# Gate sums of a product-key layer formed in PSUM: two products of 128 columns in place of one of 256, and one copy in place of copy and add

## The reference

```python
s = jnp.einsum('thpd,hpnd->thpn', q, sub_keys)            # 8 heads, 2 x 128 sub-keys
vals, idx = lax.top_k(s, K)                               # K = 16
cand = vals[:, :, 0, :, None] + vals[:, :, 1, None, :]
top_s, top_pos = lax.top_k(cand.reshape(T, PEER_HEADS, K * K), K)
experts = (i1 * PEER_NKEYS + i2).reshape(T, PEER_HEADS * K)
gates = jax.nn.softmax(top_s, axis=-1).reshape(T, PEER_HEADS * K)
a = jax.nn.gelu(jnp.einsum('td,ted->te', xb, u_tab[eb]), approximate=False)
y = jnp.einsum('te,ted->td', gb * a, v_tab[eb])
```

## Time and profile before

| | |
|---|---|
| median of 3 runs | 3389.28 us |
| the profiled execution | 3415.09 us, its span 3413.2 us |
| PE busy | 3196.7 us, 94% of the span |
| DVE busy | 2390.1 us, 70% |
| ACT busy | 1105.3 us, 32% |
| POOL busy | 997.1 us, 29% |
| sweep 1's products | 774.5 to 2276 us |
| groups of gates | 796.7 to 2039 us |

### The profile page before, as it was taken

One profiled execution on the slowest core, in us unless ns is written; L12 is line 12 of the kernel. 1 busy time (PEld: TensorE's weight loads), 2 busy tenths in 40 slices (PEclk: granted clock), 3 DMA queues, 4 the chain that ended last, 5 costly groups with the idle time before them and its releaser, 6 DMA issues. The chain is left out here.

```text
span 3413.2 us, 44800 instructions
## 1 busy us (share of the span) xinstructions
PE 3196.7 (94%) x14706; PEld 2637.1 (77%) x14706; DVE 2390.1 (70%) x4021; ACT 1105.3 (32%) x1301; POOL 997.1 (29%) x727
## 2 busy tenths in 40 slices
PE   4993999998999999999999999997998998999996
PEld 3872677887888888888888888876887886788885
DVE  5345343458878878788787873425887888888887
ACT  3123145113333333333333331122333334333333
POOL 0000010002323223232232320024554557755651
PEclk9995579999999999999999999998999999999998
DMA  6500022222333333333343333237999998999995
GB/s 243 190 30 32 1 81 99 74 80 87 146 140 129 116 134 146 140 132 117 129 152 140 139 118 133 100 142 262 352 349 352 352 360 323 372 364 355 348 362 192
DMA packets 251409, 640.91 MB, mean 188 GB/s; under 512 B 28752, under 2 KB 134352, under 8 KB 249680
## 3 DMA queue, kind: packets, MB, share of 16 engines
q1 hardware_dynamic: 205568, 503.07, 40.3%
q0 software_dynamic: 45776, 137.00, 10.7%
HBM read 505.76 MB, written 134.22 MB: 187 GB/s over the span
## 5 line engine op out<-in xcount | busy, mean ns | idle before, releaser
L1385 POOL TENSOR_TENSOR onehot<-onehot,slots 128x1024 fp32r<-128x1024 f32 x192 | 371.6, 1957 | 1183.6 <-DVE onehot L1471 1183.6
L93 PE MATMUL acc_u<-a_hi,u_hi 128*128 128x512 f32 x2048 | 633.8, 391 | 3.9 <-PEq L1110 2.5
L93 PE MATMUL acc_u<-a_lo,u_hi 128*128 128x512 f32 x2048 | 632.1, 390 | 0.0
L93 PE MATMUL acc_u<-a_hi,u_lo 128*128 128x512 f32 x2048 | 631.1, 389 | 0.0
L1873 PE MATMUL y_ps<-v_hi,c_hi 128*128 128x512 f32 x1536 | 478.2, 393 | 53.0 <-DVE c_lo L83 47.9
L78 ACT ACTIVATE v_hi<-v_raw 128x1024 fp32r<-128x1024 f32 x256 | 271.6, 1061 | 677.1 <-PE y_ps L1873 544.1
L1873 PE MATMUL y_ps<-v_lo,c_hi 128*128 128x512 f32 x1536 | 476.0, 391 | 0.0
L1873 PE MATMUL y_ps<-v_hi,c_lo 128*128 128x512 f32 x1536 | 475.7, 391 | 0.0
L83 DVE TENSOR_TENSOR v_lo<-v_raw,v_hi 128x1024 fp32r<-128x1024 f32 x256 | 316.4, 1236 | 199.8 <-ACT v_hi L78 166.5
L93 PEld LDWEIGHTS acc_u<-a_lo,u_hi 128*128 128x128 f32 x2048 | 385.0, 188 | 81.6
L93 PEld LDWEIGHTS acc_u<-a_hi,u_lo 128*128 128x128 f32 x2048 | 384.7, 188 | 80.8
(11 more groups left out here) (228 smaller groups left out, 3621.7 us busy)
## 6 DMA issues: line engine op xcount, KB each, us to landing
v_raw<-in_v SPq DMA_DIRECT2D x256, 512.0 KB
u_raw<-in_u SPq DMA_DIRECT2D x128, 512.0 KB, 3.4
act_d<-gelu SPq DMA_DIRECT2D x128, 512.0 KB, 2.6
gate_d<-gate_block SPq DMA_DIRECT2D x12, 4096.0 KB, 12.1
gt<-gate_d SPq DMA_DIRECT2D x64, 768.0 KB
at<-act_d SPq DMA_DIRECT2D x256, 192.0 KB
w_mod_b<-in_w_mod SPq DMA_DIRECT2D x6, 2560.0 KB, 9.0
w_mod<-in_w_mod SPq DMA_DIRECT2D x9, 1024.0 KB, 16.4
```

The lines of the kernel that those rows point to most:

```text
L93: done = pe.matmul(acc[:, cols], w, a[:, k, cols], start=first, stop=last)
L1385: last_op = pool.tensor_tensor(onehot_2[u][:, :, part, :], onehot_2[u][:, :, 0, :].bitcast(F32), gate.unsqueeze(2).to_broadcast([P, TOK // ...
```

## The change

The two half tables are added by PE: for each token there are now two matmuls of 128 columns, with the same stationary `onehot_1` slice, the first with `start`, the second with `stop`, into the same 128 columns of PSUM. The tile `gate_ps` is half as wide, its series is counted in 2 pieces and not in 4. ACT's copy reads the finished sum, in another order of the same elements (the experts outside, the tokens inside), and itself gives the signal `gate_out`. DVE's add and the semaphore `high_out` are gone.

```diff
-    high_out, picked = sem("high_out"), sem("picked")
+    picked = sem("picked")
-    BANKS = 4
+    BANKS = 2
-        gps_all = banks.enter_context(nc.psum_tensor("gate_ps", [P, TOK // 2, 2, NKEYS], F32))
+        gps_all = banks.enter_context(nc.psum_tensor("gate_ps", [P, TOK // 2, NKEYS], F32))
...
-            return gate_block[half][:, :, bass.ds(first, TOK // 2)].rearrange("p n t -> p t n")
+            return gate_block[half][:, :, bass.ds(first, TOK // 2)]
...
-                    act.activation(gate_columns(h, half, s), gps_all[:, :, 0, :], ACT.Copy).then_inc(high_out, 1)
+                    act.activation(gate_columns(h, half, s), gps_all[:].rearrange("p t n -> p n t"), ACT.Copy).then_inc(gate_out, 1)
...
-                def gates_out(u):
-
-                    dve.wait_ge(high_out, 2 * b + u + 1)
-                    dst = gate_columns(h, half, u)
-                    dve.tensor_tensor(dst, dst, gps_all[:, :, 1, :], ALU.add).then_inc(gate_out, 1)
-
...
-                gates_out(0)
                 split(2 * (p + 1), 0)
                 if not last:
                     compare(b + 1, (h + 1) * TOK, 0)
-                gates_out(1)
                 split(2 * (p + 1) + 1, 1)
...
-                        last = pe.matmul(gps[n][:, t % PER], onehot_1[s][:, t, :], onehot_2[s][:, t], start=True, stop=True)
+                        for part in range(2):
+                            last = pe.matmul(gps[n][:, t % PER], onehot_1[s][:, t, :], onehot_2[s][:, t, part, :],
+                                             start=part == 0, stop=part == 1)
```

More of the change, by code:

```diff
@@ L1447, in take_slots @@
                 dve.wait_ge(slots_ps, turn)
-                dve.tensor_copy(g.slots[:, 0:2, :], gps[0][:, 0, :, :])
-                dve.tensor_copy(g.slots[:, 3, :], gps[0][:, 1, 0, :]).then_inc(slots_out, 1)
+                dve.tensor_copy(g.slots[:, 0:2, :], gps[0][:, 0:2, :])
+                dve.tensor_copy(g.slots[:, 3, :], gps[0][:, 2, :]).then_inc(slots_out, 1)
                 dve.drain()
@@ L1531, in transpose_slots @@
                 for n, src in enumerate((flat(g.chosen[:, 0]), flat(g.chosen[:, 1]), flat(g.gates[:]))):
-                    last = pe.transpose(gps[0][:, n // 2, n % 2, :], src, g.ident)
+                    last = pe.transpose(gps[0][:, n, :], src, g.ident)
                 last.then_inc(slots_ps, 1)
```

## The result

The kernel after takes 3463.61 us (median of 4 runs, 3462.76 to 3464.03), the one before 3388.34 us beside it: +75.3 us, a ratio of 1.0222 with a 95% interval of 1.0204 to 1.0239. It is slower, as forecast (3469 us, 3430 to 3495).

What follows compares the result with a forecast made beforehand. PE was taken to bound sweep 1, so DVE's removed adds gain nothing in steady steps. PE's dearer gate groups, +84 us, less 4 us in the opening give +80 us: 3469 us from 3389.3, range 3430 to 3495.

Steps and rivals of the forecast that it cites:

- What bounds the kernel: Sweep 1: PE is the bound, busy 1198.59 of 1200 us; removing DVE's 248 us of adds gains nothing in steady steps.
- The price on PE: Gate groups in sweep 1: 16 matmuls of 128 columns for 8 of 256, +0.895 us a group, +84 us over 94.
- my lower bound: New gate group on PE: at least the float32 score series' 1.79 us, +0.83 us a group.
- The upper bound: New gate group on PE: at most the present price a matmul, 0.120 x 16 = 1.92 us, +0.96 us a group.
- One sign that I named: Gate matmuls in the profile after: duration 220 to 230 ns at 112 to 120 ns spacing would show the load as floor.
- The opening: Start of sweep 1, two groups without a product between: first product 3.0 us earlier, up to 4.6 with the clock, taken as 4.
- The copy on ACT: ACT's copy of the gates out of PSUM: 1.07 to 4.1 us, covered until about 10 us, so no cost.
- The sum: Whole kernel: +84 - 4 = +80 us, 3469 us for the median and 3495 us for the profiled execution.
- The load isn't the floor: Gate series on PE: a matmul costs 0.0637 to about 0.10 us, giving 3391 to 3445 us; chance 0.13.
- Done as plain float32: Gate series on PE: each narrow float32r matmul becomes two instructions, +2.62 us a group, 3631 us; chance 0.07.
- The second load is spared: Gate series on PE: each pair's second matmul needs no load, 0.94 us a group, 3383 us; chance 0.03.
- The copy comes late: Sweep 1: PE waits for ACT's copy or `u_lo` if the copy exceeds 10 us, 94 us per microsecond over; chance 0.01.

Runs made afterwards that it cites:

- e3: Kernel after, but outside the opening each gate matmul loads 64 of the 128 stationary columns; ratio 1.0000 to the kernel before.
- e7: Kernel after with the one-hot tables and both gate halves in bfloat16; ratio 0.999 to the kernel before.
- e2: Kernel after with the high half's product alone, 8 matmuls of 128 columns a group; ratio 0.9974 to the kernel before.
- e4: Kernel after with the old 8 matmuls of 256 columns and one copy of the high half, no DVE add; ratio 0.9975 to the kernel before.
- e5: Kernel after with ACT's copy in the old order of elements (tokens outside, experts inside); ratio 1.0204 to the kernel before.
- e6: Kernel before with DVE's first add of a step and the split of u behind it moved ahead of the top-16 search; ratio 1.0115.
- e1: Kernel after with the two products written to separate PSUM columns, not added, and only the high half copied; ratio 1.0225 to the kernel before.
- e9: Kernel before with bfloat16 tables and gate halves, ACT copying both halves out of PSUM, DVE adding from SBUF to SBUF; 3380.78 us, ratio 0.9982.

## Why the prediction was right, point by point

**What bounds the kernel.** Right. PE is the bound of sweep 1 and every change of its series came out in the time; 248 us off DVE gave nothing in steady steps.

**The price on PE.** Right in mechanism, and the measured price lies between my lower bound and the middle that went into the sum. I took the float32 score series as the floor, because its load is as long, and got +0.83 to +0.96 us a group, with +0.895 in the sum. Measured: the series +0.783 and the product behind it +0.084, +0.867 together, 81.5 us for 94 groups where the sum had 84. The wait of the product behind was in the bound (the 0.09 that I added to 1.70 us), and e3 with e7 showed the reason given, the load's own time. The upper bound, 0.120 us a matmul, was no floor of the load: with the same load, 8 matmuls of 128 columns follow each other every 0.111 us (e2).

**One sign that I named was wrong.** I had written that a duration of 220 to 230 ns would show the load as the floor. It was 275 ns, and the load is the floor all the same: a matmul's row begins before its load has ended and holds the wait (in the series at 1145.64 us the second matmul's row begins 57 ns behind the first, and its load ends only 134 ns after that). Only the first of a series, with its load made earlier, shows the bare 219.

**The opening.** Taken as 4 us: 3.0 for the earlier product, as worked out (it started 7.51 us behind the first series, forecast 7.5), and 1 for a clock that might be spared. The clock was not spared. What I missed is the single other wait for `u_lo`, which vanished too. Together 5 us (e4). That my 4 came so near is in part luck: 1 us in it did not come, and 1.7 us came that were not in it.

**The copy on ACT.** Covered, as argued, and shown by e5. I had left its new duration between 1.07 and 4.1 us; it is 1.03.

**The sum.** +80 us forecast, +75.3 measured in the medians and 76.7 in the two profiles' sweep 1, where 81.5 - 5 = 76.5 accounts for it. Wrong was the sentence that the sum holds for the profiled execution as well (3495 us): the one after took 3464.03 us. The profiled execution of before had lost its time in sweep 2, whose products run from 2283.3 to 3387.0 us there, 1103.7 us, and from 2360.9 to 3435.9 after, 1075.0 us; I had looked for it in sweep 1 alone.

**The rivals.** "The load isn't the floor" fell to e2 and e3. The 81 ns for 128 columns that the Trainium skill has in "TensorE: Matmul & The Clock Gate", section "Back-to-back issue gap", appeared in no run: it was 111 ns with the 4-byte load and 56 with the 2-byte one. "Done as plain float32" fell: one load and one matmul each, and 60 ns in e3. "The second load is spared" fell: 1536 loads for 1536 matmuls, also for the same stationary operand. "The copy comes late" fell to e5.

## What to carry to other kernels

In the series of this kernel a matmul costs about the longer of its stream and its load, so count loads as well as columns: splitting 256 columns of float32r in two with the same stationary operand doubles the loads, and nearly doubles the engine's price (0.95 to 1.735 us a series), while work taken off an engine that the bound one covers gives nothing. Before a sum is moved from DVE into PSUM, look whether the narrower matmul's stream is still as long as its load. With bfloat16 operands the same change cost next to nothing here (e7). And where a queue is reordered for one stall (e6), check who waits for what has moved back in all the other steps.

## What the runs showed of the hardware that I had not expected

Two matmuls in direct succession into the same PSUM columns cost the same as two into different ones (e1: 1.735 us a series in both). An ACT copy of 1024 elements from PSUM takes 1.03 us when it reads with a stride and writes runs of 8, and 2.03 us when it reads straight and writes single elements with a stride. DVE's add with one operand in PSUM and a strided output takes 2.59 us, and 1.22 us from SBUF to SBUF with the output in runs of 8 (e9). The time of the kernel before differed by 40 us, 1.2%, between batches on different chips, while the same series gave the same sweep 1 to 0.3 us (kernel after, e1 and e5) and sweep 2's products took 1075 to 1120 us.
